# Two layers of a hybrid decoder: state decays, state products and group sums of a Mamba-2 stage reordered, and the first weights of the projection behind it split in quarters

## What is computed

```python
o_inter = jnp.einsum('bthn,bhpn->bthp', cc * jnp.exp(acum)[..., None], s)
scores = jnp.einsum('bthn,bshn->btsh', cc, bc) * decay
o_intra = jnp.einsum('btsh,bshp->bthp', scores, xc)
s_new = jnp.exp(a_last)[..., None, None] * s + jnp.einsum(
    'bshn,bshp->bhpn', bc * jnp.exp(a_last[:, None] - acum)[..., None], xc)
...
y = y + d_skip[:, None].astype(xh.dtype) * xh
y = y.reshape(b, t, D_INNER_D) * jax.nn.silu(z)
y = rms_normalize(y.reshape(b, t, G_D, D_INNER_D // G_D)).reshape(b, t, D_INNER_D) * ssm_gain.astype(xn.dtype)
out = jnp.einsum('bte,ed->btd', jnp.concatenate([o_c, y], axis=-1), w_out)
```

## Time and profile before

| | |
|---|---|
| time, median of 3 | 1584.04 us (1583.19 to 1588.73) |
| time of the profiled execution | 1589.23 us |
| its span, first to last instruction | 1587.0 us |
| mean granted TensorE clock | 0.993 of full |
| TensorE matmul busy | 1556.8 us, 98% of the span |
| VectorE busy, ScalarE busy | 532.5 us, 368.5 us |
| DMA moved | 479.46 MB, mean 302 GB/s |

### The profile page before, as it was taken

The page is one execution under the profiler, slowest core; times in us unless marked ns, Lnnn a source line. Parts: engine busy times, 40 slices in busy tenths (PEclk is TensorE's granted clock), DMA queues, the critical chain, the costliest instruction groups (busy, mean ns, idle before and its releaser), DMA issues.

```text
span 1587.0 us, 37321 instructions
## 1 busy us (share of the span) xinstructions
PE 1556.8 (98%) x16801; PEld 1144.1 (72%) x16801; DVE 532.5 (34%) x783; ACT 368.5 (23%) x550; POOL 43.9 (3%) x50
## 2 busy tenths in 40 slices
PE   9989999999999999999999999999999999999997
PEld 8976799999999965953576766745746537767456
DVE  6467556564559677552101101111011011011113
ACT  4346444443427467210000000000000000000001
POOL 0000000000000000000000000000000000000000
PEclk9999999999999998999999999999999999999999
DMA  9566446543444461869899999999999999999996
GB/s 356 192 240 192 144 141 190 163 160 133 164 154 167 152 165 40 263 275 419 338 395 414 416 405 414 414 407 416 403 415 414 406 416 416 406 417 414 407 414 227
DMA packets 144488, 479.46 MB, mean 302 GB/s; under 512 B 32184, under 2 KB 61632, under 8 KB 129747
## 3 DMA queue, kind: packets, MB, share of 16 engines
q1 hardware_dynamic: 141404, 469.08, 77.2%
q0 software_dynamic: 2064, 5.66, 0.9%
q10 hardware_dynamic: 871, 2.42, 0.4%
HBM read 463.57 MB, written 13.55 MB: 301 GB/s over the span
## 4 chain that ended last, share of the span: by engine, by line
PE 56%; DVE 0%; ACT 0%; issue 0%; DVEq 0%
PE ps L2977 36%; PE ps L2993 19%; PE ps L3042 0%; PE ps L3021 0%; PE ps L229 0%; PE ps L3002 0%; PE ps L3027 0%; PE ps L3009 0%; DVE act L3201 0%; DVE act L3191 0%; DVE tail_rows L3191 0%; DVEq L2870 0%; ACT xn_tokens L3257 0%; PE ps L3031 0%; ACT item_y L3242 0%
## 5 line engine op out<-in xcount | busy, mean ns | idle before, releaser
L2977 PE MATMUL ps<-up_ring,item_x 128*32 128x448 f32 x6000 | 567.3, 539 | 0.0
L2977 PEld LDWEIGHTS ps<-up_ring,item_x 128*32 128x32 f32 x6000 | 287.3, 110 | 273.5 <-issue 198.1
L2993 PE MATMUL ps<-down_ring,hid_t 128*32 128x256 f32 x5376 | 298.8, 379 | 1.1
L2993 PEld LDWEIGHTS ps<-down_ring,hid_t 128*32 128x32 f32 x5376 | 237.7, 110 | 62.1 <-issue 10.4
L3163 DVE TENSOR_TENSOR hid<-hid,ps 128x1344 f32<-128x1344 f32 x16 | 24.9, 1554 | 662.0 <-PE ps L2977 660.6
L472 DVE TENSOR_TENSOR w_lo_dense<-ring,w_hi_dense 128x2048 fp32r<-128x2048 f32 x54 | 123.6, 2291 | 96.0 <-ACT w_hi_dense L466 96.0
L466 ACT CAST w_hi_dense<-ring 128x2048 fp32r<-128x2048 f32 x54 | 102.9, 1906 | 93.7 <-PE ps L486 86.0
L3242 ACT COPY item_y<-ps 128x512 f32<-128x512 f32 x8 | 4.7, 585 | 428.8 <-PE ps L2993 428.8
L1558 PE MATMUL ps<-x_hi_dense,w_hi_dense 128*128 128x288 f32 x352 | 94.8, 299 | 1.8 <-PEq L1422 1.8
L1559 PE MATMUL ps<-x_lo_dense,w_hi_dense 128*128 128x288 f32 x352 | 94.6, 295 | 0.0
L3238 ACT ACTIVATE hid<-ps 128x1344 f32<-128x1344 f32 x16 | 20.7, 1291 | 269.6 <-PE ps L2977 269.5
(11 more groups left out here) (507 smaller groups left out, 1745.5 us busy)
## 6 DMA issues: line engine op xcount, KB each, us to landing
up_ring<-in_we_dram SPq DMA_DIRECT2D x250, 896.0 KB, 7.6
down_ring<-in_we_dram SPq DMA_DIRECT2D x112, 1024.0 KB, 10.6
ring<-in_w_ffn_dram SPq DMA_DIRECT2D x23, 1024.0 KB, 6.9
ring<-in_w_in_odd_dram SPq DMA_DIRECT2D x9, 2048.0 KB, 7.9
ring<-in_w_in_even_dram SPq DMA_DIRECT2D x5, 2048.0 KB, 15.3
ring<-in_w_ffn_dram SPq DMA_DIRECT2D x5, 2048.0 KB, 7.7
ring<-in_w_out_odd_dram SPq DMA_DIRECT2D x3, 2048.0 KB, 8.1
odd_layer<-in_we_dram SPq DMA_DIRECT2D x6, 896.0 KB, 11.4
```

Of the source, the lines that this page charges most:

```text
L2977: mm = pe.matmul(k.ps[32 * q:32 * q + 32, 3 * w + g, 0:FW], xg[:, c, g, :], block_of[:, q, :], start=c == 0, stop=c == DC - 1, skip_group_ ...
L2993: mm = pe.matmul(k.ps[32 * q:32 * q + 32, 6 + g // 2, 256 * (g % 2):256 * (g % 2) + 256], hidT[:, 2 * r + j, g, :], block_of[:, j, 256 * q ...
```

## The change

On VectorE `decay_state` 0 to 4 move up in front of `take(4)`, decay 5 comes between `take(6)` and `take(7)`, and decays 6 and 7 after it. On TensorE the eight state products use six banks (0, 1, 2, 3, 5, 6, then 0 and 1 again) and the four sums two (4, 7, 4, 7); their order is changed, and a wait and one warm-up product are put at the end of the stage. ScalarE makes six squares in front of the first root. In `gemm_rows` the first half's weights are rounded, and their rest is taken, in quarters of 256 columns, each with a semaphore count of its own; TensorE waits for the quarter that the column block needs. Three warm-up products become one.

```diff
-    def products(self, pe, out, h, cols, rows, x, first, last, source=None):
+    def products(self, pe, out, h, cols, rows, x, first, last, source=None, lo_at=None):
...
-        self.await_lo(pe, h)
+        if lo_at:
+            pe.wait_ge(*lo_at)
+        else:
+            self.await_lo(pe, h)
...
-                    made=1 if hidden else 0, lo_made=1 if hidden else 0)
+                    made=1 if hidden else 0, lo_made=1 if hidden else 0, lead=PIECES - 1 if norm else 0, lo_lead=PIECES - 1 if norm else 0)
+        piece = lambda buf, p: buf[:, :, D // PIECES * p:D // PIECES * p + D // PIECES]
...
                 if norm:
-                    k.warm(pe, 7, 3)
+                    k.warm(pe, 7, 1)
                 for h in range(len(halves)):
-                    sp_.await_hi(pe, h)
+                    if h or not norm:
+                        sp_.await_hi(pe, h)
                     for m in range(DC):
+                        lo_at = None
+                        if norm and h == 0:
+                            pe.wait_ge(*sp_.hi_done.at(m * PIECES // DC + 1))
+                            lo_at = sp_.lo_done.at(m * PIECES // DC + 1)
...
-                    if h >= sp_.made:
+                    if norm and h == 0:
+                        act.wait_ge(*k.arrived(first))
+                        for p in range(PIECES):
+                            act.copy(piece(sp_.view(sp_.hi, 0), p), piece(halves[0][2], p)).then_inc(*sp_.hi_done.up())
+                    elif h >= sp_.made:
                         sp_.round_hi(act, h)
...
-                    if h >= sp_.made:
+                    if norm and h == 0:
+                        for p in range(PIECES):
+                            dve.wait_ge(*sp_.hi_done.at(p + 1))
+                            dve.tensor_tensor(piece(sp_.view(sp_.lo, 0), p), piece(halves[0][2], p), piece(sp_.view(sp_.hi, 0), p).bitcast(F32),
+                                              ALU.subtract).then_inc(*sp_.lo_done.up())
+                    elif h >= sp_.made:
                         sp_.take_lo(dve, h)
...
-        SUM_BANKS = (4, 7, 5, 6)
+        SUM_BANKS, STATE_BANKS = (4, 7, 4, 7), (0, 1, 2, 3, 5, 6, 0, 1)
...
-                    if i >= 4:
-                        pe.wait_ge(*n_["state_new"].at(i - 3))
+                    if i in (4, 5):
+                        pe.wait_ge(*n_["y_taken"].at(i + 3))
+                    if i >= 6:
+                        pe.wait_ge(*n_["state_new"].at(i - 5))
...
-                        pe.wait_ge(*n_["y_taken"].at(5 + g))
+                        pe.wait_ge(*n_["root"].at(2 * g - 3))
...
-                state_samples(0)
-                state_samples(1)
+                for i in range(4):
+                    state_samples(i)
                 sum_squares(0)
-                state_samples(2)
-                state_samples(3)
+                state_samples(4)
+                state_samples(5)
                 sum_squares(1)
+                state_samples(6)
+                state_samples(7)
                 sum_squares(2)
-                for i in range(4, 6):
-                    state_samples(i)
                 sum_squares(3)
-                for i in range(6, 8):
-                    state_samples(i)
+                pe.wait_ge(*n_["state_new"].at(5))
+                k.warm(pe, 5, 1)
...
+                dve.wait_ge(*n_["st_turned"].at(NB))
+                dve.wait_ge(*n_["ebc_exp"].at(1))
+                for j in range(5):
+                    decay_state(j)
                 take(4)
...
                 take(6)
-                dve.wait_ge(*n_["st_turned"].at(NB))
-                decay_state(0)
-                decay_state(1)
+                decay_state(5)
                 take(7)
-                for j in range(2, 8):
-                    decay_state(j)
+                decay_state(6)
+                decay_state(7)
...
-                for j in range(4):
+                for j in range(6):
                     square(j)
                 root(0)
-                square(4)
-                square(5)
-                root(1)
                 square(6)
                 square(7)
+                root(1)
                 root(2)
                 root(3)
```

More of the change, by code:

```diff
@@ L617, in gemm_rows @@
     half_done, added = k.count("row_half_done"), k.count("residual_added")
-    nblocks = -(-total // 4)
+    nblocks, PIECES = -(-total // 4), 4
     halves = row_halves(k, first, total)
@@ L651, in _ @@
                         mm = sp_.products(pe, k.ps[:, m, 0:T], h, slice(P * m, P * m + P), range(2 * h, 2 * h + 2), x,
-                                          h == 0, h == last, source if m == 0 else None)
+                                          h == 0, h == last, source if m == 0 else None, lo_at)
                         if h == last or m == DC - 1:
@@ L2449, in state_samples @@
                         pe.wait_ge(*ys_done.at(1))
-                    if i >= 4:
-                        pe.wait_ge(*n_["state_new"].at(i - 3))
+                    if i in (4, 5):
+                        pe.wait_ge(*n_["y_taken"].at(i + 3))
+                    if i >= 6:
+                        pe.wait_ge(*n_["state_new"].at(i - 5))
                     r = quarter(i % 4)
-                    pe.matmul(k.ps[:, i % 4, :], xs[r, 1, i // 4, :], bbd[r, i // 4, :, :], start=True, stop=True)\
+                    pe.matmul(k.ps[:, STATE_BANKS[i], :], xs[r, 1, i // 4, :], bbd[r, i // 4, :, :], start=True, stop=True)\
                       .then_inc(*n_["state_dot"].up())
@@ L2580, in new_state @@
                     dve.wait_ge(*n_["state_dot"].at(i + 2))
-                    dve.tensor_tensor(at, at, k.ps[:, i % 4, :].rearrange("p (b n) -> p b n", b=NB), ALU.add).then_inc(*n_["state_new"].up())
+                    dve.tensor_tensor(at, at, k.ps[:, STATE_BANKS[i], :].rearrange("p (b n) -> p b n", b=NB), ALU.add).then_inc(*n_["state_new"].up())
                 def take_x(n, nth):
@@ L2647, in _ @@
                 score(7)
-                dve.wait_ge(*n_["ebc_exp"].at(1))
                 dve.wait_ge(*n_["inter_dot"].at(1))
```

## The result

| | before | after |
|---|---|---|
| median of 6 runs each | 1587.74 us (1583.19 to 1589.72) | 1576.63 us (1574.61 to 1578.83) |
| profiled execution, its span | 1589.23, 1587.0 us | 1576.40, 1574.5 us |
| mean granted TensorE clock | 0.993 | 0.998 |
| VectorE, ScalarE busy | 532.5, 368.5 us | 532.0, 368.9 us |

A forecast was written before the change was run, and what follows sets the result against it. The prediction took TensorE to bound the kernel, with more than half of the span. Stage 3.9 plus projection 3.6, less 0.1, gave 7.4 us off the median 1584.04: 1576.6 us, range 1573.0 to 1581.0.

The forecast's parts named there:

- The decays and `new_state`: VectorE, state-space stage: five decays take 3.1 us inside its pause; first `new_state` at 620.65 in place of 623.66.
- the order without the decays: State-space stage, a bound: if moving the decays is worth nothing and only the order changes, the gain is 2.4 us.
- TensorE's list: TensorE, state-space stage: products and sums run from 617.59 to 626.35 without being held up; first eight passes take 2.1 us.
- The lower bound, 1.95: TensorE, first eight passes of state products at one go: 1.13 + 4 x 0.21 = 1.95 us, beside a bound of 2.12.
- The stage's gain, 3.9 us: State-space stage ends 3.9 us before 631.10: some 2.4 from waits, about 1.5 from full clock.
- The start of the projection, 3.6 us: Projection's start: with quarters, half 1 begins 7.4 us after the stage's end in place of 11.0, 3.6 less.
- The sum, 7.4 us: Whole kernel: stage 3.9 plus projection 3.6 is 7.5, less 0.1 for extra counts and waits, so 7.4 us off.
- In front of it should come off the total one for one: Experts behind the seam: nothing there is tied to a fixed time, so time saved earlier shortens the total equally.
- The last weights: Rival, projection's half 4: late weights become the wait; 2.9 us of slack, each microsecond beyond costs one; chance 0.05 with other waits.
- The clock at the new seam: Rival, border of stage and projection: TensorE's clock falls, costing 2 to 5 us; gain 3 to 6.4, chance 0.29.
- More than that: Rival: the low clock lasted longer than 10.4 us in the median's executions; 1 to 3 us more gain, chance 0.12.
- the main case: Whole kernel: 6.4 to 8.4 us gained, 1575.6 to 1577.6 us, chance 0.52.

The follow-up runs named there:

- 12: The kernel before with nothing but the five decays moved into VectorE's pause, old banks and order kept; ratio to before 0.9981.
- 5: The kernel after with the decays back where they were before, new banks, orders and quarters kept; ratio to before 1.0003.
- Experiment 8: The kernel after with state products reordered so that neighbouring products read the same group of 32 rows; ratio to before 0.9976.
- 7: The kernel after with half 0's weights rounded whole, one piece in place of four quarters; ratio to before 1.0006.
- 6: The kernel after without its two warm-up products at the seam and the wait there; ratio to before 0.9955.
- 1: The kernel before, unchanged, profiled once more; 1587.14 us, ratio 1.0005.
- 2: The kernel after, unchanged, run once more against the kernel before on the same chip; median 1577.97 us, ratio 0.9957.
- 9: The kernel after, unchanged, run once more on another chip against the kernel before there; median 1585.44 us, ratio 0.9963.

## Why the prediction was right, and what in it was off

**The decays and `new_state`.** Right. Five took 3.10 us in the pause, `take(4)` followed where TensorE's output came, and `new_state` began at +3.07 for a forecast of +3.06. The 3.0 us between this and +6.07 is worth 1.35 alone (12) and more within the new order: 5 cast at +13.53, of which 1.66 is the half clock of its last two sums, so at +11.87 or a little less at full clock, against +9.54. One bound was wrong here: the prediction gave the order without the decays 2.4 us. Experiment 5 is that kernel, and it gave 0.28 in the traces (+13.53 for +13.81, both with a fallen clock) and some 0.5 at full clock, because products 6 and 7 then wait for `new_state`.

**TensorE's list.** The order and the absence of bank waits were right. One term was mis-sized: four products at one go were taken at 2.1 us, from two groups in a row, and took 1.14. The lower bound, 1.95, was broken as well, since it rested on one pass after another. Experiment 8 shows the reason: passes in different groups of 32 rows overlap. The eight passes take 1.99 when they share two groups in place of four, and four passes take 1.98 in one group, 1.13 in two. Only part came through, since sum 0 then waited 0.54 us for its square; ScalarE ended the stage at +9.26 instead of +9.6.

**The stage's gain, 3.9 us.** It was measured against a before whose last products ran at half clock. At full clock it is 12.35 less 9.54, 2.81 us; against that execution (+13.81) it is 4.27. The prediction did price the clock, at about 1.5 (it was 1.46), and counted it as gain of the order.

**The start of the projection, 3.6 us.** The quarters did what was forecast: half 1 at 7.5 us behind the stage's end, for 7.4. The gain is 2.97 at full clock and 3.48 against the profiled execution; the same mistake, half a microsecond.

**The sum, 7.4 us.** Taken as in the prediction, it was 7.75 in the two traces. Of this 5.78 is what the order and the quarters give at full clock. The rest is clock, paid when it falls. The fitted times put that fixed part at 4.9 and 5.1, with 1 us either way, which holds 5.78. The clock was also higher over all executions of the kernel after (means 0.9961 against 0.9938 on A, 0.9951 against 0.9941 on C), which at the fitted slopes is 2.6 and 1.2 us more. Only the first of these differences is clear of noise, and 12, with hardly any gain, has as high a mean as the kernel after on A; so that the change keeps the clock up is likely from the traces and not shown by the means. The ratios give 6.8 and 5.9 us in all. So 7.4 was near because it held a part of the clock's share, as gain of the order; as that it was 1.6 too much. That the prediction's time, 1576.6, met the median of 1576.63 was luck: it set out from 1584.04, which the further runs put at 1587.74. The first comparison's 10.8 is more than either repetition, and its excess over them I can't assign; a wide spread of the kernel before, 16 us on A, allows it, and so would two chips.

**"In front of it should come off the total one for one".** Shown for the experts: from their first product to the end of the span it was 886.0 us in the kernel before and in the kernel after on chip A, and 885.8 in the first trace of the kernel after. They did not wait longer because they began earlier. The last weights did not become the wait either: SyncE's stores began at 629.07, its load at 640.32, and half 4's cast waited 3.82 us for TensorE, not for weights.

**The rivals.** The clock at the new seam stayed at 1.00 in all three traces of the kernel after, so it did not fall there in them; falls elsewhere are still in its mean. In 5 and 7, with gaps of 1.2 to 1.7 us at the seam, the clock fell there in the trace, its mean was the lowest of all (0.9928 and 0.9920), and the whole gain was gone: the rival was a real one. The fall in the trace does not explain all of it: at the fitted slope, 1.4 to 1.7 us are at most 0.0014 of the mean, and these means lie 0.002 to 0.004 below those of the kernel after on its chips. And 6 has a gap of 1.87 us, its clock fell too in its trace, and its mean was 0.9961, while 1 kept the full clock with the gaps with which the first trace of the kernel before lost it. So no single gap decides it. The rival's price was high: the prediction took up to 5 us for a fall of 10.4 us, and that fall cost 1.97, since TensorE stood idle or waited in a part of it. "More than that", which had a chance of 0.12, is what the first comparison gave, 10.8; the two repetitions gave 6.8, in the main case, and 5.9, which is in the range given to the fall of the clock, though the clock at the seam had not fallen in its trace.

**Left open.** The experts' items take 108.4 us on A and 109.3 to 109.5 on B and C, whatever the kernel. In the first trace of the kernel before, some 0.9 us are lost at one place in an item's down products. The last item, behind which no more weights have to come, took 108.42 on B and C too. Between 900 and 1500 us DMA moved 413 or 414 GB/s on A and 410 or 411 on B and C. A block of weights that comes late would do all of this; no run here took it apart.

## What to carry to other kernels

Before a gain is read out of a profile, ask which part of the old time was a low clock, and price the change at full clock: here 2 of 7.75 us were one execution's chance. Where two engines hand banks to each other, move both lists together: in the stage, at full clock, the decays alone gave 1.35 us, the new order without them some 0.5, both together 2.8. Measure such a change on one chip and against the kernel before there, since chips here differed by as much as the change is worth.

## What the runs showed of the hardware

Products of 32 rows by 512 columns run at the same time when they read different groups of 32 rows: eight passes took 1.14 us over four groups and 1.99 over two, and two passes more in a group cost 0.85, so passes in one group follow 0.43 apart. The Trainium skill, "TensorEngine Tiling (Array Packing)" (Tiling Modes, Key Properties), says that tiles work independently of each other and are tied to their partitions; the traces agree with the first of these by 1.14 against 1.99.

Falls of the clock cost like amounts here: from half 1 to the experts' first product it was 50.8 to 51.1 us in the two traces without one, 52.4 to 52.8 with one, and 54.2 or 54.3 with two, so some 1.6 us each; at the seam a fall cost 1.4 to 1.7 (5, 6, 7 and 12) and the long one of the kernel before 1.97. Whether it falls is a matter of the execution: the same kernel after had one fall on that way in two traces and two in the third.

Chips differ in the experts' loop: the same instructions took 108.43 us an item on one and 109.3 to 109.5 on two others, and the stage from its first product on 886.0 against 892.6 us (experiments 2 and 9), as much as this change is worth. All but the last item of a chip's run carry the difference.
